# Attention of one fox head a step, 16 steps a tile instead of 12

## The reference, cut to what matters

```python
def _fox_attn(q, k, v, cq, ck, qpos, kpos):
    s = jnp.einsum("bqhd,bkhd->bhqk", q, k).astype(jnp.float32) * (DK_B ** -0.5)
    s = s + jnp.transpose(cq, (0, 2, 1))[..., :, None] - jnp.transpose(ck, (0, 2, 1))[..., None, :]
    mask = kpos[None, :] <= qpos[:, None]
    p = jax.nn.softmax(jnp.where(mask, s, NEG), axis=-1)
    return jnp.einsum("bhqk,bkhd->bqhd", p.astype(v.dtype), v)
...
    oa = _rmsnorm(oa, subln_g) * (1.0 - lambda_init)
    ya = jnp.einsum("bte,ed->btd", oa.reshape(bsz, t, VA_W), w_pa)
    yb = jnp.einsum("bte,ed->btd", ob.reshape(bsz, t, VB_W), w_pb)
    merged = gates[:, :, 0] * ya + gates[:, :, 1] * yb
    x = x + jnp.einsum("btd,de->bte", merged, w_o)
    x = x + _peer(_rmsnorm(x, norm2_g), peer_wq, peer_subkeys, peer_u, peer_v)
```

## Time and profile before

| | |
|---|---|
| time, median of 3 runs | 2459.55 us (2457.28 to 2459.71) |
| the profiled execution | 2440.04 us, its span 2438.2 us |
| mean granted TensorE clock | 0.88 |
| PE busy | 1917.0 us, 79% |
| DVE busy | 1510.4 us, 62% |
| ACT busy | 596.1 us, 24% |
| DMA | 765.00 MB, mean 314 GB/s |
| ACT_TABLE_LOAD | 67 of them ahead of gelus alone (86.0 us) |

### The profile page before, as it was taken

How to read it: one execution, slowest core, us unless ns; L and a number is a source line. 1 busy time by engine, 2 the same in 40 slices (tenths; PEclk the granted TensorE clock), 3 DMA queues, 4 the chain that set the end, 5 groups by cost and what they waited for, 6 DMA issues and landing times. The chain is left out here.

```text
span 2438.2 us, 22936 instructions
## 1 busy us (share of the span) xinstructions
PE 1917.0 (79%) x7392; PEld 1124.0 (46%) x7392; DVE 1510.4 (62%) x3470; ACT 596.1 (24%) x1631; POOL 723.1 (30%) x697
## 2 busy tenths in 40 slices
PE   7989897899896876996787689858776788787655
PEld 6855674457544642443562234446432334553211
DVE  0021208786655478867659876655797655758956
ACT  3231011311241122532122244301222332013211
POOL 0000000443323133324234533322344223334533
PEclk9988999999977998978899998789988777899888
DMA  7831654999869777879999977699998665999987
GB/s 248 299 111 52 194 203 143 418 421 398 317 273 339 310 303 284 318 270 362 410 404 398 378 292 295 269 394 404 419 364 355 258 240 220 410 413 389 355 324 298
DMA packets 139303, 765.00 MB, mean 314 GB/s; under 512 B 18608, under 2 KB 42464, under 8 KB 52016
## 3 DMA queue, kind: packets, MB, share of 16 engines
q0 software_dynamic: 78336, 570.46, 59.1%
q1 hardware_dynamic: 27632, 161.42, 17.6%
q10 hardware_dynamic: 33216, 31.67, 4.0%
HBM read 744.77 MB, written 18.30 MB: 313 GB/s over the span
## 5 line engine op out<-in xcount | busy, mean ns | idle before, releaser
L646 POOL DMA_INDIRECT ring<-in_uv,stage x544 | 668.7, 1229 | 1249.5 <-issue 384.4
L1259 PE MATMUL acc<-ring,diag 128*128 128x512 f32 (+1 forms) x1268 | 706.2, 709 | 235.4 <-DVE diag L1593 119.1
L1582 DVE CUSTOM_DVE_ANT_0 ring<-ring,xb 128x1024 f32<-128x1024 f32 x544 | 648.6, 1220 | 137.3 <-DMA ring<-in_uv,stage 120.3
L1259 PEld LDWEIGHTS acc<-ring,diag 128*128 128x128 f32 (+1 forms) x1268 | 267.0, 221 | 626.0 <-issue 303.5
L920 ACT ACTIVATE gel<-dots 128x1 f32<-128x1 f32 x544 | 102.5, 200 | 892.8 <-DVE dots L1582 877.5
L1607 DVE SCALAR_TENSOR_TENSOR vsum<-ring,coefd,vsum 128x1024 f32<-128x1024 f32 x222 | 285.3, 1285 | 8.8 <-DVE coefd L1600 0.8
L1034 PE MATMUL pz<-F,wbuf 128*128 128x416 f32 (+1 forms) x656 | 243.0, 530 | 24.4 <-ACT F L781 19.0
L1034 PEld LDWEIGHTS pz<-F,wbuf 128*128 128x128 f32 (+1 forms) x656 | 125.6, 194 | 137.8 <-issue 137.8
L664 POOL COPY stage<-idx 128x4 int32<-128x4 int32 x136 | 51.7, 380 | 437.9 <-DVE gw L1538 417.9
L1600 DVE TENSOR_SCALAR coefd<-gel,gw 128x1 f32<-128x1 f32 x227 | 47.5, 209 | 143.3 <-ACT gel L920 142.9
L1593 DVE TENSOR_SCALAR diag<-ident,gel,gw 128x128 f32<-128x128 f32 x159 | 54.8, 353 | 99.7 <-ACT gel L920 97.4
(11 more groups left out here) (312 smaller groups left out, 2185.2 us busy)
## 6 DMA issues: line engine op xcount, KB each, us to landing
wbuf<-in_w_z SPq DMA_DIRECT2D x52, 1024.0 KB
wbuf<-in_w_q SPq DMA_DIRECT2D x40, 1024.0 KB
wbuf<-in_w_pa SPq DMA_DIRECT2D x20, 1024.0 KB
wbuf<-in_w_o SPq DMA_DIRECT2D x20, 1024.0 KB
wbuf<-in_w_pb SPq DMA_DIRECT2D x20, 512.0 KB
ring<-in_uv,stage POOLq DMA_INDIRECT x544
zT<-F ACTq DMA_DIRECT2D x28, 208.0 KB, 5.3
wbuf<-in_w_sk SPq DMA_DIRECT2D x5, 1024.0 KB
```

The costliest lines, as they stand in the source:

```text
L646: pool.indirect_dma_start(out=ring[:, slot, :], out_offset=None, in_=d["uv"], in_offset=bass.IndirectOffsetOnAxis(ap=stage[:, a, k:k + 1], ...
L1259: last = nc.tensor.matmul(acc[0:nq, c * 512:(c + 1) * 512], diag[:, parity, 0:nq], ring[:, slot, D + c * 512:D + (c + 1) * 512], start=Fal ...
L1582: nc.vector.tensor_tensor_reduce(out=u, in0=u, in1=xb[:, t % 2, :], scale=1.0, scalar=0.0, op0=ALU.mult, op1=ALU.add, accum_out=dots[:, sl ...
```

## The change

`STEPS` gets one fox head a step: eight steps with one fox head each stand where four with two stood, so a tile has 16 steps and, with the two that run out, 18 pieces of attention instead of 14. `weight_of` gives 3.0 instead of 5.0 to the pieces after the first eight, so that these weigh 30 as before (ten of 3.0, six of 5.0), and nothing outside the fox heads moves in tiles 1 to 4 against the half-blocks. In the front of tile 0 the weights of `wait_of` stay 5.0 a piece, so there the projection's chunks move by a few pieces. Which slots are added by PE and which by DVE stays as it was, and no instruction of computation is added or removed.

```diff
--- before.py
+++ after.py
@@ -89,7 +89,7 @@
 
 
 
-STEPS = [[v] for v in range(8)] + [[v, v + 1] for v in range(8, 16, 2)]
+STEPS = [[v] for v in range(16)]
 
 ATTEND, NORM_O, TURN_O = 1, 1 + len(STEPS) + 2, 2 + len(STEPS) + 2
 YPROJ = TURN_O + 1
@@ -131,7 +131,7 @@
     if p == 0:
         return 12.0 if i == TILES - 1 else 4.0
     if ATTEND <= p < NORM_O:
-        return 5.0
+        return 5.0 if p - ATTEND < 8 else 3.0
     if p >= TOP:
         return 6.0
     if OPROJ <= p < NORM_X or QPROJ <= p < SCORE:
```

## The result

The changed kernel took 2469.38 us (median of 20 runs, 2453.54 to 2474.24), the kernel before 2451.07 us in its 20 runs (2442.11 to 2460.39). The ratio is 1.0058, 95% interval 1.0041 to 1.0076: some 14 us slower by the ratio (the two medians lie 18.3 us apart), where 5.8 us faster was forecast.

The account below looks back on a forecast made before the run. PE was taken to set the pace of the fox steps, where gathers wait. Terms -10.8 + 4.0 + 3.0 - 2.0 = -5.8 us, laid on the median 2459.55, gave 2453.7 us, range 2434 to 2474.

Parts of the forecast that it names:

- The other moves: Front of tile 0: projection chunks come some pieces later, but PE works through the same queue without waiting; 0 us.
- The clock: Fox steps, all tiles: shorter stretches win back part of the granted clock; -10.8 us, 7.3 of it in tiles 2, 3.
- The hole more in tile 4: Tile 4 fox steps: every head now waits like the first of a pair, four times 1.43 - 0.43; +4.0 us.
- Table loads: ACT: 20 more loads of 1.28 us, mostly hidden because PE is behind; +3 us, bounds 0 and 25.7.
- the rival in which the chain takes the lead: One-head steps: PE waits at each copy; up to 2487 us, half the loads 2476; chance 0.15.
- The refill: After the clumps of tiles 2 and 3: spread work fills some of PE's idle time at the empty ring; -2 us.
- The other signs: Profile after: POOL's longest waits in tile 3 under 8 us; DMA share falling in fox steps would mean the chain.

## Why the prediction was wrong

- **The other moves, the step that failed.** The prediction set the chunks of tile 0 at 0, because PE works through the same queue of work there. PE's work is the same, but what stands beside it isn't: from the subkey scores on the front of tile 0 runs on DVE's top-k for 38 us to L1512 and 15 more to L1536, and PE's chunks are free there, while a chunk among the query projections costs its length. The weights of `wait_of` went from 70 to 90 for attention, and that moved one chunk of 11.4 us out from under this cover. It was measured by itself at 1.0055, some 13 us, against 1.0058 for the whole change, and the first dot moved by 11.8 us on average. I had listed that chunks move, and did not ask past which engine's work.
- **The clock** went the way forecast where one step stands in a gap: in the four traces with one head in each gap in tiles 2 and 3 and fewer than five chunks, it was 0.82 to 0.88 in tile 2's fox steps and 0.83 in tile 3's, against 0.83 to 0.87 forecast and 0.78 and 0.75 before. That the spacing by adds does it, rather than the scores themselves, was tried and held. The size forecast for these two was 7.3 us; with the output projections 4.7 us came in tile 3 and about 2, within the spread, in tile 2. The 3.5 us in tiles 0, 1 and 4 did not come: with the chunks back the first dot is at 287.5 us, as with pairs, tile 1 took 232.9 us before and 232.8 after from half-block 31 to 51, and in tile 4 the clock was 0.67 in two traces with one head and 0.74 in the changed kernel, for 0.73.
- **The hole more in tile 4** was right in kind. There are three more of about 1 us and not four, since the last head has no exponential ahead of its copy: 2.7 us in place of 4.0. The steps lost 7.7 us in the two runs with one head there and the exponentials first, three chunks in place, and there PE's idle time did not grow at all: the loss is PE's longer busy time, with the clock at 0.67. In the changed kernel they lost 4.6 us, 2.6 in busy and 2.0 in idle time, with the clock at 0.74, so the cause of the loss in tile 4 stays in part open.
- **Table loads.** All 20 came. No run changed them alone, but in tiles 2 and 3 the hole ahead of a head's values stayed at 0.58 and 0.69 us with them, so they are covered there, as argued, and the rival in which the chain takes the lead is out. In tile 4 the reordered copies brought one-head steps level with pairs with every table load in place. The 3 us can't be seen.
- **The refill** can't be told from the clock; whatever it brought is in the 4.7 us.
- **The other signs.** The gathers did start sooner in tile 3, but POOL's longest wait for a slot there, 10.58 us before, was 9.21 and not under 8. DMA's share rose in the fox steps of tiles 2 and 3 and stayed at 0.56 in tile 4's, which is not the sign of the chain.
- The sum without the failed step, -5.8 us, agrees with the run that has all one-head steps and the chunks in place, 0.9984 or -4 us. With an interval of -11 to +3 that is weak support, and partly luck: tile 4 is worse than taken, and the terms of tiles 0 and 1 and the table loads, which did not show, have opposite signs.
- A slip that changed nothing: by the prediction's own terms half of the table loads on the path give 2474, not 2476.

## What to carry to other kernels

A list of weights that deals work out moves more than the work whose weight is changed: print the new order on the engine that takes the moved work, and ask of each piece that moved which engine's work it ran under. A piece with a free place under another engine's long serial stretch can cost its whole length elsewhere, as here among the query projections, and the wait where the engines meet again at the end of that stretch tells how it is filled: the cover's partner idle for 12.71 us with a chunk too few, the long engine itself for 7.44 with one too many. A shorter stretch with gathers beside it can lose part of its gain in the stretch behind it, where the DMA is full: read both windows together. And date the same landmark in several traces before a difference between two of them is explained: of the 17.2 us here between two traces, some 5 were within the spread.

## What the runs showed of the hardware

The granted clock differed with how the same matmuls are spaced: in tile 3, the same heads and the same adds ran at 0.83 with adds behind every head, at 0.76 and 0.75 with adds behind every second, PE being busy for 86 to 91% in all three. The spacing is not all: in the three traces with five chunks ahead, the same stretch of tile 3 had 0.83 with pairs and 0.89 and 0.91 with one head. In tile 4 a hole of up to 1.48 us ahead of seven heads' values went with 0.67 in two traces and with 0.74 in a third, where pairs had 0.73, and holes of 0.9 us with 0.76, so that here no rule follows.

A load of ACT's function table took 1.28 us on average of all, and 12 more of them in tiles 2 and 3 left the holes of 0.58 and 0.69 us ahead of a head's values there as they were.
